# Expert stages that ask for their queries piecemeal, modulation kept as columns, decays by Relu on ScalarE

## The chip, the core and the metric

One core of one Trainium2 chip runs the whole program. The metric is device microseconds of one execution, from its first to its last instruction and what lies around them. TensorE is called PE, VectorE DVE, ScalarE ACT, GpSimd POOL; SP is the engine that issues most of the transfers. Everything is float32.

## What is computed

The reference chains two blocks over a sequence of 256 tokens of width 1024 (two tiles of 128 tokens, tt = 0 and 1 below). The first block has two layers of a hybrid mixer (four retention heads, and a state space part, SSD, with 32 heads in four groups) and a swiglu layer. The second block has two layers too; it has a second input, a context of 256 tokens:

```python
m_x = _modulation(c, w_mod[l], b_mod[l])                 # six rows of 1024: shift, scale, gate, twice
h = _modulate(x, norm1_g[l], m_x[0], m_x[1])             # rmsnorm(x) * g * (1 + scale) + shift
mix_x, _ = _token_mix(h, lp, ang, kv_c)                  # attention, Fourier and pooling branches
x = x + m_x[2] * mix_x
h2 = _modulate(x, norm2_g[l], m_x[3], m_x[4])
x = x + m_x[5] * _peer(h2, w_pq[l], peer_keys[l], peer_down[l], peer_up[l])
```

The context goes through the same in layer 0, and gives only keys and values in layer 1. `_peer` is the expert stage: eight query heads per token score 2 x 128 keys, the best 16 pairs of a head name 16 experts, and so a token has 128 experts; of each a row of `peer_down` (dotted with h2) and a row of `peer_up` (added up, weighted by gate times gelu of the dot product) are fetched. In the SSD part a head's decay matrix is exp(min(seg, 0)), seg being a difference of cumulative sums, times a masked product.

## The kernel before

`Plan.order` writes one list of items; each engine's program walks that list and emits its own part of every item, so an engine's instructions stand in the order of the list, and an engine that waits holds all that stands behind. Two streams are woven into the list. `x_stream` runs the first block, then for both layers of the second block `mix_phase` (modulation and token mix of x) and `peer_x` (expert stage of x). `context_stream` runs `modulation` (the product of c with `w_mod`, 48 MB), the context's `mix_phase` and its expert stage `peer_c`. Each generator yields an estimate of time, and `streams` takes the next item from the stream that is behind; at "alone" the context stream is emptied into the list. No instruction is moved at run time.

`modulation` (L635) adds up two rows per part in a PSUM bank, DVE adds the bias (L1813) and SP stores the rows to DRAM, in `mods` (L2356). `modulate` (L687) is called before each token mix and each expert stage: SP loads the norm gain, the scale and the shift as rows broadcast to 128 partitions (`mod_load`, L2366), DVE makes (1 + scale) * gain (L1819), and for either token tile multiplies by 1/rms and that gain (L1824) and adds the shift (L1826); PE turns the tile in blocks of 128 x 128 (L1214) and ACT copies four blocks at a time to `hT` (L2181). 1/rms comes by squares on ACT (L2081), a small step on DVE (L1615) and one on POOL (L2302). In the mixer, the rotation table is loaded behind `hT` (`load_cs`, L2370), and SP loads the first weights (wkv) behind that.

The first block's norms go by `stats`, `scaled`, `turn` (L313 to 326): squares, scaling on ACT (L2095), turning on PE (L1214) and a multiply on DVE into `hT` (L1623). PE fills the wait for them with products that nothing reads (`keep_busy`, L1224). `mix_out` adds the mixer's output to x on DVE (L1777), the second half of swiglu is added at L1790.

`heads` is the SSD part of one pair of heads: PE makes cumulative sums in a bank (L1300), DVE subtracts and takes the minimum with 0, three operations of 128 x 128 a head (L1706 to 1708), ACT takes the exponential (L2133), DVE multiplies by step and mask (L1713, L1714), PE multiplies by the inputs (L1290 to 1292). Each layer has 16 such pairs.

`peer_c` brings rows of one expert half at a time and uses DVE for both: dot products (`down`, L2013) and sums (`up`, L2024). `peer_x` first does all eight queries (`query`: 32 matmuls, L1179, then a copy by ACT, L2254) and scores (`score`, 8 matmuls, L1551; copies L2260 and L2261). Ranking (`rank`, L1909 to L1962, on DVE) makes one head's 16 indices. Then 256 steps follow, n = 128 tt + k: POOL fetches down and up row of expert k of each of the 128 tokens, 1 MB, into a ring place (L2315, q0 of the profile), DVE does the dot product (L2013); four steps make a batch, whose gelu is done at once (L1985 to L1992, L2269), ACT makes a diagonal matrix per expert (L2279) and PE adds the up rows by it in two banks (L1561, four matmul records per expert). A place comes free when its PE sums have ended. In layer 0 the ring has 11 places, of which the last three (wx[2], hT, keys) come free when all queries and scores have ended; in layer 1 it has 14. Beside the steps of layer 0, `context_keys` makes the context's keys and values for layer 1, in the steps from n = 60 on, one piece every ten.

```python
        for i in range(9):
            if i < 8:
                query(i, early[i] if i < 3 else None)
            if i:
                score(i - 1)
```

## Time and profile before

| what | value |
|---|---|
| time, median of 3 runs | 4311.15 us (4305.10 to 4315.73) |
| the profiled execution's time | 4306.61 us |
| its span | 4305.2 us |
| granted PE clock, mean | 0.938 |
| PE busy | 3722.5 us, 86% |
| DVE busy | 2369.1 us, 55% |
| POOL busy | 1300.6 us, 30% |
| ACT busy | 601.2 us, 14% |
| read from HBM | 1211.07 MB, 282 GB/s |
| first block | to about 2236 us |
| x, layer 0: token mix; expert stage | 2236 to 2548; 2548 to 3294 us |
| x, layer 1: token mix; expert stage | 3294 to 3577; 3577 to 4305 us |

Busy shares are over the whole span, and the stages differ: in the token mixes PE is nearly always busy, in the expert stages of x the transfers are. The time of a stage is read from the engine or queue that ends last in it. In rows of the timeline, what stands in brackets is how long the engine had been idle, and what released it.

### The profile page before, as it was taken

What the parts mean: (1) busy time and instruction counts of PE and PEld (TensorE: products, weight loads), DVE (VectorE), ACT (ScalarE), POOL (GpSimd) and SP (SyncE); (2) the same over time, 40 slices, a digit from 0 to 9 for tenths busy, and PEclk for the clock granted to TensorE, in tenths of its full rate; (3) what the DMA queues carried; (4) which work ended last, traced back from release to release, by engine and by line L of the source; (5) the groups of instructions that cost most, each with busy time, mean ns of one, the idle gap of its engine ahead of it and who ended that gap; (6) DMA issues with size and microseconds to landing.
All of it is one profiled execution on the core that took longest, in us unless ns stands there. A gap on an engine that the chain in (4) does not pass through costs nothing. (4 is left out here: it accounts for less than half of the span.)

```text
span 4305.2 us, 41073 instructions
## 1 busy us (share of the span) xinstructions
PE 3722.5 (86%) x14696; PEld 2637.1 (61%) x14696; DVE 2369.1 (55%) x5573; ACT 601.2 (14%) x1567; POOL 1300.6 (30%) x1125
## 2 busy tenths in 40 slices
PE   8978899997988679999988998877877999877777
PEld 6667788886847568887846775333334787333333
DVE  3542112367767876766762115777774122877875
ACT  1212100100001110000002101111111221111111
POOL 1100000001664445765640003444441001444442
PEclk9989999998998879999998999998998999899999
DMA  8652334333997769999962338999996235999997
GB/s 322 248 207 97 125 139 184 139 138 125 413 367 283 251 236 363 405 398 366 408 265 90 118 134 355 418 374 382 419 421 256 108 113 227 391 421 421 421 421 317
DMA packets 209546, 1214.93 MB, mean 282 GB/s; under 512 B 23889, under 2 KB 25041, under 8 KB 97729
## 3 DMA queue, kind: packets, MB, share of 16 engines
q0 software_dynamic: 154368, 855.71, 49.7%
q1 hardware_dynamic: 54976, 356.60, 21.9%
q8 instruction: 119, 1.95, 0.2%
q14 instruction: 83, 0.67, 0.0%
HBM read 1211.07 MB, written 1.15 MB: 282 GB/s over the span
## 5 line engine op out<-in xcount | busy, mean ns | idle before, releaser
L1179 PE MATMUL bank<-big 128*128 128x256 f32 (+3 forms) x9848 | 2144.1, 378 | 68.9 <-issue 14.8
L1179 PEld LDWEIGHTS bank<-big 128*128 128x128 f32 x9848 | 1836.8, 192 | 379.0 <-issue 91.8
L2315 POOL DMA_INDIRECT big<-in_pboth,big x1024 | 1230.1, 1201 | 1279.3 <-PE bank L1561 635.4
L1561 PE MATMUL bank<-big 128*128 128x512 f32 x2048 | 1007.6, 651 | 278.4 <-ACT big L2279 278.3
L2013 DVE CUSTOM_DVE_ANT_0 big<-big 128x1024 f32<-128x1024 f32 x768 | 926.9, 1224 | 334.7 <-DMA big<-in_pboth,big 331.0
L1561 PEld LDWEIGHTS bank<-big 128*128 128x128 f32 x2048 | 416.6, 208 | 866.5 <-issue 501.3
L2302 POOL TENSOR_TENSOR big<-big 128x1 f32<-128x1 f32 (+1 forms) x49 | 44.6, 912 | 1565.6 <-DVE big L1615 1565.5
L2024 DVE SCALAR_TENSOR_TENSOR big<-big 128x1024 f32<-128x1024 f32 x254 | 326.2, 1284 | 36.3 <-DMA big<-in_pboth,big 12.9
L2279 ACT ACTIVATE big<-big 128x128 f32<-128x128 f32 x512 | 164.8, 391 | 251.6 <-DVE big L1992 241.5
L1214 PE MATMUL bank<-big 128*128 128x128 f32 x572 | 97.9, 309 | 96.6 <-DVE big L1826 37.7
L1214 PEld LDWEIGHTS bank<-big 128*128 128x128 f32 x572 | 75.7, 161 | 117.2 <-issue 68.3
L2269 ACT ACTIVATE big<-big 128x4 f32<-128x4 f32 x128 | 26.4, 207 | 767.6 <-DVE big L1988 767.6
L1688 DVE SCALAR_TENSOR_TENSOR big<-big,bank 128x512 f32<-128x512 f32 x32 | 22.0, 687 | 188.3 <-ACT big L2121 188.3
L1891 DVE SCALAR_TENSOR_TENSOR big<-big,bank 128x512 f32<-128x512 f32 x36 | 24.8, 689 | 177.2 <-PE bank L1179 177.1
L1869 DVE TENSOR_REDUCE big<-bank 128x1 f32<-128x512 f32 (+1 forms) x48 | 28.9, 603 | 164.8 <-PE bank L1462 163.9
L1369 PE MATMUL bank<-big 128*128 128x512 f32 x256 | 112.5, 601 | 7.3 <-DVE big L1784 7.3
L1224 PE MATMUL bank<-big 128*128 128x256 f32 x296 | 73.9, 411 | 40.8 <-DVE big L1623 29.0
L1672 DVE SCALAR_TENSOR_TENSOR big<-bank,big 128x255 f32<-128x255 f32 (+1 forms) x144 | 62.8, 478 | 79.8 <-ACT big L2109 78.1
L1224 PEld LDWEIGHTS bank<-big 128*128 128x128 f32 x296 | 61.1, 209 | 52.2 <-DVE big L1623 29.7
L1369 PEld LDWEIGHTS bank<-big 128*128 128x128 f32 x256 | 49.1, 193 | 69.8 <-issue 61.8
L2081 ACT ACTIVATE big<-big 128x1024 f32<-128x1024 f32 x26 | 27.5, 1056 | 415.0 <-DVE big L1790 148.7
L1770 DVE SCALAR_TENSOR_TENSOR big<-big,bank 128x256 f32<-128x256 f32 x32 | 13.5, 421 | 125.0 <-PE bank L1179 125.0
(197 smaller groups left out, 2167.4 us busy)
## 6 DMA issues: line engine op xcount, KB each, us to landing
big<-in_w SPq DMA_DIRECT2D x104, 1024.0 KB, 7.3
big<-in_wmod POOLq DMA_DIRECT2D x48, 1024.0 KB, 9.1
big<-in_wgu SPq DMA_DIRECT2D x44, 1024.0 KB, 8.0
big<-in_wzg SPq DMA_DIRECT2D x36, 1024.0 KB, 4.8
big<-in_wro SPq DMA_DIRECT2D x32, 1024.0 KB, 6.8
big<-in_wpq SPq DMA_DIRECT2D x24, 1024.0 KB, 4.8
big<-in_wd SPq DMA_DIRECT2D x22, 1024.0 KB, 8.0
big<-in_pboth,big POOLq DMA_INDIRECT x1024, 12.4
```

What stands on the lines that cost most here:

```text
L1179: last = pe.matmul(o, a, b, start=(i == 0), stop=(i == n - 1))
L1214: last = pe.transpose(o[:, i, :], b, ident)
L1224: pe.matmul(u.ap[:, 0:256], ident, p.masks, start=True, stop=True)
L1369: last = pe.matmul(us[2 * tt + n].ap, act[:, 2 * i + k, tt * P:tt * P + P], wk[:, k, 512 * n:512 * n + 512], start=(i + k == 0), stop=False)
L1561: last = pe.matmul(u.ap, d.ap, row[:, 512 * i:512 * i + 512], start=(k == 0), stop=(k == 127))
L1672: i = v.scalar_tensor_tensor(c[:, m, s:256], o[:, m, 0:256 - s], conv["w"][m][:, 3 - s:4 - s], c[:, m, s:256], ALU.mult, ALU.add)
L1869: step(v.reduce_max(sm[:, c:c + 1], u.ap[:, 0:nk * P], AX.X))
L2013: v.tensor_tensor_reduce(row, row, h, 1.0, 0.0, ALU.mult, ALU.add, out).then_inc(done[0], 1)
L2024: v.scalar_tensor_tensor(at, s.ap, by, at, ALU.mult, ALU.add).then_inc(done[0], 1)
L2279: s.activation(d.ap, p.ident, ACT.Copy, scale=by).then_inc(diag[0], 1)
L2302: g.tensor_tensor(r.sm[:, 8 + r.at:8 + r.at + r.n], r.sm[:, 4 + r.at:4 + r.at + r.n], r.sm[:, 12:13].to_broadcast([P, r.n]), ALU.pow).then ...
L2315: g.indirect_dma_start(out=s.ap, out_offset=None, in_=table, in_offset=bass.IndirectOffsetOnAxis(ap=index, axis=0)).then_inc(s.full[0], 16)
```

## The change

1. **Expert stages of x.** Query 0, score 0 and query 1 are placed first, then the ranking of head 0 with its gates, then score 1, query 2, score 2. Queries 3 to 7 stand in front of the steps n = 8, 20, 32, 44 and 56, their scores in front of n = 10, 22, 34, 46 and 58. At n = 60, wx[2], hT and keys join the ring. In layer 0 four places are lent to the ring from the room of `context_keys`, and given back from n = 40 on; the pieces of `context_keys` come every twelve steps from n = 72. Two of the kernel's own places serve first as room for modulation rows. The ring has 11 places at the start of layer 0, 7 after n = 40 and 10 from n = 60 on, and 10, then 13, in layer 1.
2. **Last gates.** The last eight steps of a stage form batches of 2, 2, 2, 1 and 1 instead of two of 4.
3. **Modulation as columns.** `modulation` also turns each part by four blocks on PE (`mod_columns`) and keeps shift and gain as columns. `modulate` scales tile 0 by 1/rms on ACT and tile 1 on DVE, PE turns, and ACT and DVE each take four blocks of a tile with gain and shift as they copy to `hT`. The first norm needs no rows from DRAM. The expert stages still need rows of h2 for the dot products: they are loaded and made apart (`modulated_rows`), after the ranking of head 0 in x and after `hT` in the context. SP asks for keys ahead of them, and for the rotation table behind x instead of behind `hT`.
4. **Decays.** The three operations a head of DVE become ACT's Relu with scale -1, and the exponential has scale -1.
5. **Places in the list.** After `mix_out` and after the last add of swiglu, statistics, both turns and the scaling of tile 1 stand together, and the time that the stream yields comes behind them.

```diff
+    def modulate(self, banks, sm, X, l, vec, which, h, hT, room=None):
...
+        put("row_scale", src=X[:, 0, :], dst=h[:, 0, :], by=sm[:, 8:9], r=rs[0], done=done[0], ready=ready)
+        put("row_scale_v", src=X[:, 1, :], dst=h[:, 1, :], by=sm[:, 9:10], r=rs[1], done=done[1])
...
+        for tt in range(2):
+            us = [banks.take() for _ in range(2)]
+            put("col_turn", h=h[:, tt, :], us=us, dst=hT[:, :, tt * P:(tt + 1) * P], done=done[tt], gain=gain, shift=shift,
+                cols_ok=self.cols_ok, r=None if vec or tt else rs[0])
...
-            put("load_cs", cs=cs, done=tick("d_cs", 16), before=[hT_ok])
+            self.put("load_cs", cs=cs, done=cs_ok, before=[self.x_ok])
...
+        asking = ask()
+        route = ranks(asking)
+        for _ in range(3):
+            next(asking)
+        for _ in range(6):
+            next(route)
+        for _ in range(3):
+            next(asking)
+        rows_ok = yield from rows(hT_ok)
...
+        brief = [] if last else pairs[-len(spare):]
...
+                if slot in brief and n >= 40:
+                    brief.remove(slot)
+                    self.side_ok = done
...
+        ends = {(tt, k) for tt, k in steps if k % 4 == 3} | {(1, k) for k in (121, 125, 126)}
...
+            if n < 60 and n % 12 in (8, 10):
+                next(asking)
+            if n == 60:
+                for _ in asking:
+                    pass
+                asked_all()
...
-            if n >= 60 and n % 10 == 0:
+            if n >= 72 and n % 12 == 0:
...
-            v.tensor_scalar(d.ap[:, 0, :], pa.ap[:, o:o + 128], acs[:, 0, h:h + 1], 0.0, ALU.subtract, ALU.min)
+            s.activation(d.ap[:, 0, :], pa.ap[:, o:o + 128], ACT.Relu, bias=acs[:, 0, h:h + 1], scale=-1.0)
```

PE's order where the expert stage of layer 0 begins. wx0 to wx2 are the query weights' places, free4 and free5 the emptying of the banks, d_keys_x the keys' transfer. Before:

```order
L1179 MATMUL bank4<-big 128x256 [waits wx0,free4,free0]
L1179 MATMUL bank4<-big 128x256 x15
L1179 MATMUL bank5<-big 128x256 [waits wx1,free5]
L1179 MATMUL bank5<-big 128x256 x15
L1551 MATMUL bank4<-big 128x128 [waits free4,d_keys_x]
L1551 MATMUL bank4<-big 128x128 x3
L1179 MATMUL bank5<-big 128x256 [waits wx2,free5]
```

Now, in the change's own line numbers (L1257 is a query's product, L1634 a score's, L1644 the up sum):

```order
L1257 MATMUL bank4<-big 128x256 [waits free4,wx0,free0,free5]
L1257 MATMUL bank4<-big 128x256 x15
L1634 MATMUL bank5<-big 128x128 [waits free4,d_keys_x,free5]
L1634 MATMUL bank5<-big 128x128 x3
L1257 MATMUL bank4<-big 128x256 [waits wx1,free4]
L1257 MATMUL bank4<-big 128x256 x15
L1634 MATMUL bank5<-big 128x128 [waits free4,free5]
```

Score 0 stood behind query 1 and stands behind query 0. Before, five more queries and six more scores came ahead of the first up sum (L1561); now the fourth query comes behind four up sums, as the same engine's rows a little further on show:

```order
L1644 MATMUL bank0<-big 128x512 [waits pair2,diag_done]
L1644 MATMUL bank1<-big 128x512
L1644 MATMUL bank0<-big 128x512 [waits pair3,diag_done]
L1644 MATMUL bank1<-big 128x512
L1257 MATMUL bank4<-big 128x256 [waits wx0,free4]
L1257 MATMUL bank4<-big 128x256 x15
L1644 MATMUL bank0<-big 128x512 [waits pair4,diag_done]
```

DVE's order behind the last `mix_out` of the first block's second layer (L1777; full3 is its bank). L2024 are sums of the context's expert stage, L1623 the multiplies that empty the turned blocks. Before:

```order
L1777 SCALAR_TENSOR_TENSOR big<-bank,big 128x512 [waits full3]
L1615 TENSOR_SCALAR big<-big 128x1 [waits squares_done]
L2024 SCALAR_TENSOR_TENSOR big<-big 128x1024 [waits rows_read,row1,act_done_c]
L2024 SCALAR_TENSOR_TENSOR big<-big 128x1024 [waits rows_read,row2,act_done_c]
L2024 SCALAR_TENSOR_TENSOR big<-big 128x1024 [waits rows_read,row3,act_done_c]
L1623 TENSOR_TENSOR big<-bank,big 128x4x128 [waits full4]
L1623 TENSOR_TENSOR big<-bank,big 128x4x128 [waits full5]
```

Now (L1851 is `mix_out`, L1706 the multiply, L2133 the context's sum):

```order
L1851 SCALAR_TENSOR_TENSOR big<-bank,big 128x512 [waits full3]
L1698 TENSOR_SCALAR big<-big 128x1 [waits squares_done]
L1706 TENSOR_TENSOR big<-bank,big 128x4x128 [waits full4]
L1706 TENSOR_TENSOR big<-bank,big 128x4x128 [waits full5]
L1706 TENSOR_TENSOR big<-bank,big 128x4x128 [waits full4]
L1706 TENSOR_TENSOR big<-bank,big 128x4x128 [waits full5]
L2133 SCALAR_TENSOR_TENSOR big<-big 128x1024 [waits rows_read,row1,act_done_c]
```

The context's sums went from between the statistics and the two turns to behind both turns.

## Rows read from the trace of the kernel before

**Rows 1.** The page: rate of the transfers in 40 slices of 107.6 us.

```profile
GB/s 322 248 207 97 125 139 184 139 138 125 413 367 283 251 236 363 405 398 366 408 265 90 118 134 355 418 374 382 419 421 256 108 113 227 391 421 421 421 421 317
```

**Rows 2.** Windows of 10 us, expert stages: length, PE, PEld, DVE, ACT, POOL, clock, DMA share, GB/s.

```profile
2610.00:2620.00 10.00, 10.00 (x54) 8.90 (x54) 0.00 (x0) 1.70 (x4) 0.95 (x1) 1.00 1.02 422
2620.00:2630.00 10.00, 9.33 (x51) 8.14 (x50) 0.00 (x0) 2.64 (x9) 1.33 (x2) 1.00 0.21 72
...
2880.00:2890.00 10.00, 7.87 (x42) 5.27 (x41) 0.17 (x1) 1.06 (x6) 1.01 (x2) 1.00 0.52 216
...
2930.00:2940.00 10.00, 10.00 (x21) 4.38 (x20) 9.48 (x27) 1.59 (x6) 6.50 (x5) 0.84 0.61 213
...
3660.00:3670.00 10.00, 7.79 (x13) 3.46 (x14) 9.35 (x33) 1.28 (x4) 1.89 (x2) 0.66 0.76 277
```

**Rows 3.** Time to landing of the expert fetches: 2640 to 2860, 2585 to 2640, 3700 to 4250 us.

```profile
DMA to landing us min/median/max: 6.1/12.4/16.0
...
DMA to landing us min/median/max: 5.6/11.1/19.9
...
DMA to landing us min/median/max: 10.8/20.9/24.6
```

**Rows 4.** Timeline from the end of layer 0's token mix to the first fetch.

```profile
2548.31 1.06 ACT L2081 ACTIVATE big<-big 128x1024 f32<-128x1024 f32 x1 [37.16 <-DVE big L1905]
2560.83 1.97 PE L1214 MATMUL bank<-big 128*128 128x128 f32 x8 [5.88 <-DVE big L1826]
2565.69 14.14 PE L1179 MATMUL bank<-big 128*128 128x256 f32 x64 [0.68 <-ACT big L2181]
2581.51 0.29 DVE L1909 MAX8 big<-big 128x8 f32<-128x128 f32 x1 [18.28 <-ACT big L2261]
2591.81 1.00 POOL L2315 DMA_INDIRECT big<-in_pboth,big  x1 [40.03 <-DVE big L1962]
```

**Rows 5.** Timeline: layer 1's last two batches of up sums, and its last dot product.

```profile
4280.52 8.84 PE L1561 MATMUL bank<-big 128*128 128x512 f32 x16 [2.79 <-ACT big L2279]
4289.83 7.15 PE L1561 MATMUL bank<-big 128*128 128x512 f32 x16 [0.48 <-ACT big L2279]
...
4287.14 1.23 DVE L2013 CUSTOM_DVE_ANT_0 big<-big 128x1024 f32<-128x1024 f32 x1 [1.25 <-DMA big<-in_pboth,big]
```

**Rows 6.** Timeline: PE at the first weights of the token mixes of layers 0 and 1.

```profile
2264.28 5.40 PE L1179 MATMUL bank<-big 128*128 128x128 f32 x32 [5.48 <-DMA big<-in_wkv]
3305.15 1.90 PE L1214 MATMUL bank<-big 128*128 128x128 f32 x8 [4.56 <-DVE big L1826]
3314.59 5.88 PE L1179 MATMUL bank<-big 128*128 128x128 f32 x32 [4.95 <-DMA big<-in_wkv]
```

**Rows 7.** Timeline: PE's waits in the first block, behind the norms.

```profile
1032.23 6.14 PE L1224 MATMUL bank<-big 128*128 128x256 f32 x20 [15.43 <-DVE big L1623]
1285.06 6.01 PE L1224 MATMUL bank<-big 128*128 128x256 f32 x20 [7.61 <-DVE big L1623]
1992.19 7.42 PE L1224 MATMUL bank<-big 128*128 128x256 f32 x20 [5.96 <-DVE big L1623]
```

**Rows 8.** The SSD heads: lines of the page and of its groups by form, and PE's wait.

```profile
L1706 DVE TENSOR_SCALAR big<-bank,big 128x128 f32<-128x128 f32 x64 | 22.2, 346 | 38.4 <-PE bank L1300 33.2 <-DVE big L1696 3.8 <-issue 1.3
L2081 ACT ACTIVATE big<-bank 128x128 f32<-128x128 f32 x8 | 2.1, 273 | 34.6 <-PE bank L1179 34.6
L2279 ACT ACTIVATE big<-big 128x128 f32<-128x128 f32 x512 | 164.8, 391 | 251.6 <-DVE big L1992 241.5 <-PE bank L1561 10.0
1544.12 0.69 PE L1290 MATMUL bank<-big 128*128 128x64 f32 x2 [7.63 <-DVE big L1714]
1500.00:1600.00 100.00, 71.66 (x352) 63.03 (x352) 76.16 (x129) 17.11 (x35) 44.19 (x37) 0.80 0.70 238
```

**Rows 9.** Timeline: PE where the modulation has ended.

```profile
300.75 9.24 PE L1179 MATMUL bank<-big 128*128 128x256 f32 x32 [9.50 <-DMA big<-in_w]
314.08 1.07 PE L1214 MATMUL bank<-big 128*128 128x128 f32 x8 [4.09 <-DVE big L1826]
```

More of the change, by code:

```diff
@@ L503, in first_block @@
             yield from group_inputs(0, gots[0])
-            put("dt_sums", u=self.pa2.take(), dts=dts, ready=la_ok)
+            dts_ok = tick("dt_summed")
+            put("dt_sums", u=self.pa2.take(), dts=dts, ready=la_ok, done=dts_ok)
             for g in range(4):
@@ L647, in modulation, with part_end @@
         coming, late = [], []
+        def part_end():
+            l, part, args = late.pop()
+            put("mod_store", **args)
+            u = Use(banks.banks[(3 * l + part) % 2])
+            self.cols_ok = u.free
+            c4 = self.mcols[:, 2 * l:2 * l + 2, 16 * part:16 * part + 16].rearrange("p v (j b) -> p v j b", j=4)
+            gains = [(self.gcols[:, 4 * l + 2 * v + part // 2, :], self.mcols[:, 2 * l + v, 8 + 24 * (part // 2):16 + 24 * (part // 2)],
+                      self.col[l, "n2" if part else "n1"]) for v in range(2)] if part != 1 else []
+            put("mod_columns", src=args["rows"], u=u, ready=args["ready"], dst=c4, gains=gains)
         yield 30
@@ L650, in modulation @@
             for part in range(3):
-                s, b, u = st.take(), self.load(bm, t["bmod"][l, part], 512), banks.take(full=False)
+                s, b, u = st.take(), self.load(bm, t["bmod"][l, part], 512), Use(banks.banks[(3 * l + part) % 2], full=False)
                 put("mod_bias", ws=[b])
@@ L670, in modulation @@
                 rows = self.mods[l].rearrange("v a d -> v (a d)")
-                late.append(dict(dst=[rows[:, 2048 * part + 512 * j:2048 * part + 512 * j + 512] for j in range(4)],
-                    src=[s.ap[32 * j:32 * j + 2, :] for j in range(4)], ready=u.free, done=stored[turn]))
-        put("mod_store", **late.pop())
+                late.append((l, part, dict(rows=s.ap, dst=[rows[:, 2048 * part + 512 * j:2048 * part + 512 * j + 512] for j in range(4)],
+                    src=[s.ap[32 * j:32 * j + 2, :] for j in range(4)], ready=u.free, done=stored[turn])))
+        part_end()
         for w in few:
@@ L1086, in more, with lend, asked_all @@
             free.append(s)
-        while ar.size - ar.at >= 2048:
-            more(ar.get(2048))
+        for ap in places[:-2]:
+            more(ap)
         for ap in spare:
             more(ap)
+        brief = [] if last else pairs[-len(spare):]
         lent = []
-        for w in (self.wx[3], self.wx[4], self.wx[2]):
+        def lend(w):
             more(w.ap, w.freed)
             lent.append((w, pairs[-1]))
-        more(hT.rearrange("p a b -> p (a b)"), ended["hT"])
-        more(keys.rearrange("p a b -> p (a b)"), ended["keys"])
+        lend(self.wx[3])
+        lend(self.wx[4])
+        for ap in places[-2:]:
+            more(ap, rows_ok)
+        def asked_all():
+            put("load_row", dst=m5, src=self.mods[l, 0, 5:6, :].to_broadcast([P, 1024]), done=m5_ok, before=[ended["keys"]])
+            lend(self.wx[2])
+            more(hT.rearrange("p a b -> p (a b)"), ended["hT"])
+            more(keys.rearrange("p a b -> p (a b)"), ended["keys"])
         steps = [(tt, k) for tt in range(2) for k in range(128)]
@@ L1392, in mod, with mod_columns, col_turn @@
                              stop=(k == 7), tile_position=(0, 32 * j)).then_inc(done[0], 1)
-    def mod_turn(h, us, done, r=None, **_):
+    def mod_columns(src, u, ready, **_):
+        opened(u)
+        pe.wait_ge(*ready)
+        turn(u, [src[:, b * P:b * P + P] for b in range(4)]).then_inc(u.full[0], 1)
+    def col_turn(h, us, done, r=None, **_):
         for g, u in enumerate(us):
@@ L1406, in low_rank @@
         opened(u)
-        if ready:
-            pe.wait_ge(*ready)
+        for ok in ready or ():
+            pe.wait_ge(*ok)
         pe.wait_ge(*ws[0].full)
@@ L1538, in peer_q @@
     def peer_q(w, u, hT, ready, **_):
-        if ready:
-            pe.wait_ge(*ready)
+        for ok in ready or ():
+            pe.wait_ge(*ok)
         channel_chunk(u, w, hT)
@@ L2085, in halves, with row_stats, row_scale @@
         return [x[:, 0, :], x[:, 1, :]]
-    def row_stats(src, dump, r, ready):
+    def row_stats(src, dump, r, ready, room=None):
+        for ok in (ready, room):
+            if ok:
+                s.wait_ge(*ok)
+        squares(r, [src], [dump])
+    def row_scale(src, dst, by, r, done, ready=None):
         if ready:
             s.wait_ge(*ready)
-        squares(r, [src], [dump])
-    def row_scale(src, dst, by, r, done):
         s.wait_ge(*r.done)
@@ L2176, in mod_c, with col_turn @@
         s.activation(c3, c2, ACT.Tanh, scale=0.5).then_inc(tanh[0], 1)
-    def mod_turn(us, dst, **_):
-        for g, u in enumerate(us):
-            s.wait_ge(*u.full)
-            s.copy(dst[:, 4 * g:4 * g + 4, :], turned(u, 4)).then_inc(u.free[0], 1)
+    def col_turn(us, dst, gain, shift, cols_ok, **_):
+        u = us[0]
+        s.wait_ge(*cols_ok)
+        s.wait_ge(*u.full)
+        for k in range(4):
+            i = s.activation(dst[:, k, :], turned(u, 4)[:, k, :], ACT.Identity, bias=shift[:, k:k + 1], scale=gain[:, k:k + 1])
+        i.then_inc(u.free[0], 1)
     def low_rank(n, u, tmp, r, scaled, **_):
```

213 lines of the change are left out of this document (133 added, 80 removed).

## The prediction

> **What bounds the kernel now.** I read the page first. The transfers run at 421 GB/s in some slices of both expert stages of x and at 90 to 260 elsewhere [rows 1]: two of those slices are full, and nothing but fewer bytes or fewer gaps shortens them. So I cut these stages into windows of 10 us and looked for gaps [rows 2]. In layer 0 there is one at 2620 to 2630 us, where the rate falls to 72 GB/s, and the windows from 2880 to 2950 fall to between 213 and 398. Against 421 these cost about 9 us (with the window behind the first) and 21 us; small dips at 2790 and 2810 cost 3. In layer 1 the windows from 3650 to 3690 lose 8 us together, the worst stands in rows 2. Third, the landing times of the fetches [rows 3]: the shortest is 5.6 us with little queued, the median 12.4 us in layer 0 (11 places) and 20.9 in layer 1 (14). The three places more are 8.5 us, 2.8 a place, close to the 2.5 us that 1.05 MB take at 421 GB/s. What a landing takes above 5.6 us is the queue's reserve: 6.8 us in layer 0. Fourth, the way to the first fetch [rows 4]: 43.5 us from the end of the token mix (2548.3) to 2591.8, in which the transfers do little. Last, waits of PE outside these stages [rows 6 to 9], where PE is busy nine tenths of the time and a wait of PE is a loss unless the same place has another behind it.
>
> The sum is made against the profiled execution, 4306.6 us; the median of the runs is 4.5 us above it.
>
> **The way to the first fetch.** Before, squares end at 2549.5, the rows wait for their loads, hT is full at 2565.6, two queries of 7.1 us and a score pass before ranking starts at 2581.5, which takes 10.3 us [rows 4]. Now: squares and root of tile 0 to +2.1 us, ACT has the squares of tile 1 too (+2.7), scaling 1.1 (+3.8), eight turns 2.0, the same for tile 1, and four blocks copied at the end by ACT and DVE at 0.3 each: hT at +9.1 instead of +17.3, 8.2 us less. Score 0 stands behind one query: 7.2 less, 1.2 back for the copy between them that PE now waits for, 6.0 less. First fetch **14.2 us earlier** in each layer. DVE then makes the h2 rows in five operations of 1.25 us; the first row lands 5.6 us after its issue, so the first dot product is some 2 us late, and the ring covers that.
>
> **Behind the first fetch, layer 0.** The gap at 2620 was a full ring while PE worked off eight queries. It goes (9 us less), and ten route pieces in ten steps on DVE bring back some 2. Each query put between the steps takes PE 7.2 us and a score 1.1. A batch of four needs 7.15 us of PE at full clock [rows 5] per 10 us of transfers, so the batch behind a query starts 4.4 us late and the next but one is in time; the reserve of 6.8 us covers this. After n = 40 the ring has 7 places. Then one batch's places come free over 7 us, a fetch lands 5.6 us later, and the next batch closes only when the row behind it has been read: about 11.7 us a batch instead of 10. Five batches are 8.5 us, two of them with a query in front add 3.5: 12 more. From n = 60 there are 10 places against 11, so the two stalls by the context's keys (21 us) lose 2 more each: 4 more. Its three loads of 0.5 MB are gone: 3.7 less. Some weights now load behind the first fetch instead of before it, 1 MB: 2.5 more. Last gates: the last dot product ends at 4288.4 and PE at 4297.0 [rows 5]; with batches of 2, 2, 2, 1, 1 PE follows the rows at 1.8 us each and ends at about 4294, 3 less. Layer 0: 14.2 + 7 + 3.7 + 3 - 12 - 4 - 2.5 = **9.5 us less**.
>
> **Layer 1.** No places are given back; 10 places until n = 60 leave a landing of about 10.9 us, 5.3 above the shortest, still over 4.4. 14.2 + (8 - 2) + 3 - 2.5 = **21 us less**.
>
> **Start of the token mixes.** In layer 0 the order on DVE still has five of the context's sums and its last add in front, so only 3.3 us of the modulation go; the rotation table no longer holds wkv back, 5 of the 5.48 us wait: **8 us less**. In layer 1 [rows 6] x is ready at 3294.5 and PE starts at 3314.6; now hT is full at +9.1 and wkv, asked for at 3294.5, has landed: **11 us less**.
>
> **The first block's turns.** PE's bank is opened by L1623, which stood behind the context's work. Without that work DVE could have run it 6.5, 5.6 and 4.0 us earlier than it did in the three waits [rows 7]: **16 us less**. The context's work is only moved behind; DVE has room for it, at 60 to 70% busy there. If PE stands at the next bank instead, up to all of it comes back.
>
> **The decays.** 384 operations of 346 ns leave DVE [rows 8], 192 a layer. They overlap, and a pair of heads holds DVE for 1.9 us. In layer 0 DVE is half idle and I count nothing. In layer 1 PE waits four times for L1714, 2.4 to 7.6 us each; 2 of each and two waits of 1.5 us behind L1708 are 11 us. If DVE's own load set the pace, each of four groups would be shorter by what left it, 8 us, 33 in all. The windows there have DVE at 76 and PE at 72%: they wait for each other in turn. I take **20 us less**, between 11 and 33. What ACT takes on is hidden: it is 17% busy there. Its price for a Relu from a bank has no row; the nearest, a squares pass of the same shape from a bank, has 273 ns, and a scaled copy between SBUF places 391.
> The Trainium skill, ScalarE: Activation LUTs, section Rules for kernel authors, says of relu "Use VectorE, not ScalarE", since DVE is up to about three times as fast per element in bf16. The rows are of float32 from a bank, with 273 ns for ACT and 346 for DVE, so the trace does not agree for this shape. By the rule, a pair on ACT would take 5.7 us instead of 1.9, and 32 pairs 122 us more than now if nothing hid them.
>
> **The end of the modulation.** The weights for which PE waited 9.5 us [rows 9] stood behind three loads of 0.5 MB and are asked for 1.3 us earlier: 5 less. The context's rows, 4.1 and 1.4 us of waits: 5.5 less. 24 more turns on PE, at 1.1 to 2 us for eight: 4 more. **6.5 us less.**
>
> **Sum.** 9.5 + 21 + 8 + 11 + 16 + 20 + 6.5 = 92 us; 4306.6 - 92 = **4214 us**, own range 4190 to 4240.
>
> **Rivals.**
> *The ring is short.* For it: in layer 0 the reserve was once down to half a microsecond (shortest landing 6.1 against 5.6), and seven places are four fewer. Against: a median of 12.4. If each of ten insertions loses 3 us and the 20 steps with 7 places lose 30 instead of 12, the time is 4214 + 30 + 18 = **4262**.
> *The first block keeps its time.* The turns and decays only uncover the next wait (8.3 us for L1733 and 6 for the root stand beside them): 28 of the 36 us come back, **4242**.
> *Relu is the dearer.* At 391 ns a piece, unhidden, the pair loses 6 x 0.13 us against DVE's pace, 25 us over 32 pairs, and the 20 are lost: **4259**. The rule above points this way; the row of 273 ns speaks against it.
> *More than forecast.* Decays give 33, and the stalls by the context's keys lose nothing from the lost place and the 7 places nothing: **4185**.
> *Slower: PE becomes the bound of the first 60 steps.* Its place is the up sums with a query between them. At the lower level of the clock (1.2 GHz) a query takes 13.7 us, a score 2.2 and, at 8.84 us a batch [rows 5] (the batch that stands first there; part of it ran at that level, behind 2.8 us of idling), twelve steps 42 us against 30. It decides from the point where PE's twelve steps pass 30 us. Ten times 12.3 is 123 us more: 4214 + 123 = **4337**. Against it: the batch with little idling before it took 7.15 us, and PE with queries idles less, and in the window 2610 to 2620 with queries back to back the granted clock was 1.00.
> The Trainium skill, TensorE: Matmul & The Clock Gate, section What's actually happening, states that activity releases the throttle; the trace agrees, with a granted clock of 1.00 at 2610 and of 0.66 at 3660 [rows 2].
> That the change does not do what it says I leave out: the order on the engines shows it.
>
> **How the numbers follow.** Forecast 0.50, ring short 0.20, first block 0.12, Relu 0.03, more 0.11, slower 0.04. Of the time, 4175 to 4280 holds all but the slower case and the tails of the outer ones, about 0.85 by this count, a little under that for what I did not think of. A measurement of this kernel tells 0.3%, 13 us, from no change. All cases but the last are faster by more; a tail of the ring case, with twice its loss, comes to no change. Faster 0.92, same 0.04, slower 0.04.
>
> **What would show it.** First fetches some 14 us after the start of the stages less than before, 29 instead of 43.5 from the end of the token mix. No window under 300 GB/s between the first fetch and n = 40. Windows of 350 to 400 GB/s while there are 7 places. In layer 1, PE's product with wkv 9 us behind x. The waits for L1623 under 9, 3 and 3 us. PE at 80% instead of 72% in layer 1's heads. I am wrong if fetches land in 6 us over long stretches outside the seven-place steps, if PE's waits in the first block keep their sum under other names, or if the clock in the first 60 steps falls below 0.8.

## The result, and the profile after

The changed kernel takes **4274.4 us** (median; 4271.2 to 4276.1) where the kernel before takes 4312.2: ratio 0.9911, 95% interval 0.9895 to 0.9927, so 38 us faster, between 31 and 45. The forecast was 92 us, 4214 us in a range of 4190 to 4240. The profiled execution took 4274.6 us against 4306.6.

The page of the changed kernel, its busy times and its 40 slices of 106.8 us (transfers in GB/s):

```profile
PE 3683.7 (86%) x14648; PEld 2608.6 (61%) x14648; DVE 2322.7 (54%) x5464; ACT 658.6 (15%) x1800; POOL 1299.2 (30%) x1125
...
GB/s 325 236 198 106 120 148 169 146 117 144 413 370 312 265 254 386 405 402 386 411 231 62 137 206 383 308 384 311 403 416 300 108 114 262 380 402 420 420 420 336
```

Against [rows 1]: where slices 25 to 28 ran at 355, 418, 374 and 382, they run at 383, 308, 384 and 311. Layer 0's expert stage has holes that it did not have. Two marks of the timeline cut the program into stages: the squares passes that follow each sum into x, and the first expert fetch of each layer. Differences of these marks, in us (before and after are the profiled executions; the other rows are the experiments below):

| | mixer 0 | swiglu 0 | mixer 1 | swiglu 1 | token mix 0 | to first fetch | experts 0 | token mix 1 | to first fetch | experts 1 |
|---|---|---|---|---|---|---|---|---|---|---|
| before | 1003.9 | 263.2 | 705.2 | 264.0 | 312.0 | 43.5 | 702.7 | 281.2 | 43.5 | 679.9 |
| after | 1008.9 | 250.6 | 684.6 | 258.8 | 303.2 | 27.8 | 745.8 | 270.7 | 27.8 | 688.7 |
| forecast of the difference | -6.5 | -36 in these three | | | -8 | -14.2 | +4.7 | -11 | -14.2 | -6.5 |
| measured | +5.0 | -12.6 | -20.6 | -5.2 | -8.8 | -15.7 | **+43.1** | -10.5 | -15.7 | **+8.8** |
| e1, places back late | 1008.5 | 250.5 | 691.9 | 258.8 | 302.8 | 27.8 | 725.4 | 270.8 | 27.8 | 691.5 |
| e2, turns on ACT | 1006.9 | 250.6 | 689.1 | 260.5 | 303.4 | 27.8 | 728.1 | 270.9 | 28.1 | 689.1 |
| e3, score placed | 1010.0 | 250.6 | 688.4 | 258.8 | 302.8 | 27.8 | 734.5 | 270.8 | 27.9 | 683.5 |
| e4, Relu alone | 1006.3 | 264.5 | 696.9 | 263.5 | 314.6 | 43.7 | 703.6 | 282.7 | 45.4 | 680.7 |
| e5, decays on DVE | 1003.5 | 250.6 | 701.9 | 258.5 | 303.3 | 27.8 | 740.4 | 271.4 | 27.9 | 689.5 |
| e6, turns apart | 1009.0 | 263.0 | 698.9 | 266.5 | 309.6 | 27.8 | 741.2 | 271.0 | 27.9 | 689.7 |
| e7, three edits | 1006.8 | 250.6 | 687.7 | 258.8 | 303.2 | 27.9 | 699.6 | 271.8 | 28.1 | 682.2 |
| e9, Relu in layer 1 only | 1003.8 | 250.6 | 684.6 | 258.5 | 300.4 | 27.8 | 697.2 | 270.4 | 27.8 | 679.5 |
| e10, load ahead | 1006.0 | 258.7 | 695.3 | 258.7 | 307.6 | 27.8 | 698.1 | 272.7 | 27.9 | 682.4 |

(+4.7 is the forecast of -9.5 without the -14.2 that has its own column.) Outside the two columns of the expert stages the first mixer missed its forecast by 11.5 us, and the rest came near it; behind the first fetches 38 us were lost in layer 0 and 15 in layer 1 against it. Three views of the changed kernel show how.

**First**, windows of 10 us of layer 0 (columns as in [rows 2]), and the timeline around the hole:

```profile
2660.00:2670.00 10.00, 10.00 (x18) 4.27 (x19) 9.02 (x29) 0.94 (x4) 0.00 (x0) 0.71 0.44 184
2670.00:2680.00 10.00, 8.97 (x37) 6.62 (x36) 0.00 (x0) 1.76 (x5) 0.00 (x0) 1.00 0.00 0
...
2690.00:2700.00 10.00, 9.23 (x15) 4.04 (x16) 4.23 (x15) 1.28 (x4) 3.09 (x3) 0.68 0.55 205
...
2850.00:2860.00 10.00, 6.73 (x12) 2.98 (x13) 9.59 (x27) 2.85 (x10) 1.68 (x2) 0.66 0.31 107
...
2890.00:2900.00 10.00, 10.00 (x19) 4.16 (x18) 8.37 (x23) 1.64 (x7) 5.10 (x4) 0.78 0.42 136
```

```profile
2655.70 0.94 POOL L2442 DMA_INDIRECT big<-in_pboth,big  x1 [0.70 <-PE bank L1644]
2659.74 10.10 PE L1644 MATMUL bank<-big 128*128 128x512 f32 x16 [4.31 <-ACT big L2406]
2669.68 7.09 PE L1257 MATMUL bank<-big 128*128 128x256 f32 x32
2676.86 0.59 ACT L2381 COPY big<-bank 128x512 f32<-128x512 f32 x1 [13.31 <-PE bank L1257]
2677.35 1.27 ACT L2406 ACTIVATE big<-big 128x128 f32<-128x128 f32 x4
2677.80 7.15 PE L1644 MATMUL bank<-big 128*128 128x512 f32 x16 [1.03 <-ACT big L2406]
2680.06 0.94 POOL L2442 DMA_INDIRECT big<-in_pboth,big  x1 [23.42 <-PE bank L1644]
```

The sums that end at 2669.8 free four places, and all four are the lent ones, which go to nobody. The next batch waits behind a query on PE, and its diagonals (L2406) behind the query's copy (L2381) on ACT. POOL idles 23.4 us and the transfers stop. From there to n = 60 the first fetches of the batches stand at 2680.1, 2694.8, 2710.9, 2726.0 and 2741.3: 15 us a batch, where the forecast worked out 11.7.

**Second**, the gaps at 2850 and 2890, from the same timeline (this list ends at 2900.00, inside the sums that begin at 2889.22):

```profile
2842.83 1.37 DVE L1934 TENSOR_SCALAR big<-bank,big 128x128 f32<-128x128 f32 x4 [7.41 <-PE bank L1292]
2853.27 15.81 PE L1644 MATMUL bank<-big 128*128 128x512 f32 x32 [10.55 <-ACT big L2406]
2857.55 0.95 POOL L2442 DMA_INDIRECT big<-in_pboth,big  x1 [14.24 <-PE bank L1644]
...
2879.35 1.37 DVE L1934 TENSOR_SCALAR big<-bank,big 128x128 f32<-128x128 f32 x4 [6.91 <-PE bank L1292]
2889.22 11.01 PE L1644 MATMUL bank<-big 128*128 128x512 f32 x19 [9.99 <-ACT big L2406]
2893.28 1.95 POOL L2442 DMA_INDIRECT big<-in_pboth,big  x1 [13.70 <-PE bank L1644]
```

L1934 is DVE's half of the context's turned blocks. The turn (L1292) stands on PE behind a batch of sums, so DVE waits for PE with the next dot products queued behind; when they are done, PE has idled 10 us and POOL 14. Before, ACT alone emptied these banks.

**Third**, DVE's waits for ACT's tanh (L2396) in a batch's gelu, in layer 1:

```profile
3694.00 0.16 DVE L2101 SCALAR_TENSOR_TENSOR big<-big 128x4 f32<-128x4 f32 x1 [4.57 <-ACT big L2396]
3731.76 0.16 DVE L2101 SCALAR_TENSOR_TENSOR big<-big 128x4 f32<-128x4 f32 x1 [8.46 <-ACT big L2396]
```

The rows of ACT and PE just before the first of these two:

```profile
3692.12 1.05 PE L1634 MATMUL bank<-big 128*128 128x128 f32 x8
3693.21 0.37 ACT L2387 COPY big<-bank 128x256 f32<-128x256 f32 x1 [7.25 <-PE bank L1634]
3693.74 0.22 ACT L2396 ACTIVATE big<-big 128x4 f32<-128x4 f32 x1
```

ACT is not busy there: the copy of a score (L2387) stands ahead of the tanh and waits for PE, which has the query's delay and a batch of sums ahead of the score (L1634).

In the first block, the waits that answer to [rows 7], [rows 9] and [rows 8] (the list of rows ends at 300.00 for the row at 298.84, so its 1.62 us are part of the product):

```profile
1030.44 6.41 PE L1302 MATMUL bank<-big 128*128 128x256 f32 x20 [8.04 <-DVE big L1706]
1271.78 6.27 PE L1302 MATMUL bank<-big 128*128 128x256 f32 x20 [1.88 <-DVE big L1706]
1959.91 4.58 PE L1302 MATMUL bank<-big 128*128 128x256 f32 x20 [1.88 <-DVE big L1706]
...
298.84 1.62 PE L1257 MATMUL bank<-big 128*128 128x256 f32 x3 [3.92 <-DMA big<-in_w]
736.50 9.20 PE L1257 MATMUL bank<-big 128*128 128x256 f32 x32 [8.09 <-DMA big<-in_w]
...
1519.25 0.69 PE L1368 MATMUL bank<-big 128*128 128x64 f32 x2 [6.07 <-DVE big L1788]
```

The turns' waits fell by 17 us together, the weights' wait at the end of the modulation by 5.6, and a new one of 8.1 us stands at 736.5. The decays' wait fell from 7.63 to 6.07, and with the three others of its layer from 22.6 to 18.3 us together.

### The profile page after: what moved, and what is told of

It reads as the page before. It is cut to its first block and busy times, and to the rows that moved or that the text cites. A ratio compares the mean times of both kernels' runs of the same rounds, so it can differ in the third digit from the quotient of the medians.

```text
span 4273.1 us, 41154 instructions
## 1 busy us (share of the span) xinstructions
PE 3683.7 (86%) x14648; PEld 2608.6 (61%) x14648; DVE 2322.7 (54%) x5464; ACT 658.6 (15%) x1800; POOL 1299.2 (30%) x1125
## 5 line engine op out<-in xcount | busy, mean ns | idle before, releaser
L1257 PE MATMUL bank<-big 128*128 128x256 f32 (+3 forms) x9848 | 2143.7, 378 | 65.3 <-DMA big<-in_w 15.9
L1257 PEld LDWEIGHTS bank<-big 128*128 128x128 f32 x9848 | 1837.3, 192 | 379.1 <-issue 87.5
L1644 PE MATMUL bank<-big 128*128 128x512 f32 x2048 | 998.3, 645 | 323.2 <-ACT big L2406 322.0
L1644 PEld LDWEIGHTS bank<-big 128*128 128x128 f32 x2048 | 412.4, 206 | 895.6 <-issue 492.4
L2133 DVE SCALAR_TENSOR_TENSOR big<-big 128x1024 f32<-128x1024 f32 x254 | 326.1, 1284 | 36.9 <-DMA big<-in_pboth,big 14.1
L2406 ACT ACTIVATE big<-big 128x128 f32<-128x128 f32 x512 | 165.0, 391 | 239.8 <-DVE big L2101 234.7
L1292 PE MATMUL bank<-big 128*128 128x128 f32 x596 | 94.3, 294 | 75.3 <-ACT big L2208 24.9
L2396 ACT ACTIVATE big<-big 128x4 f32<-128x4 f32 (+2 forms) x134 | 27.7, 207 | 740.4 <-DVE big L2097 735.9
L1292 PEld LDWEIGHTS bank<-big 128*128 128x128 f32 x596 | 73.6, 152 | 96.6 <-issue 76.5
L1447 PE MATMUL bank<-big 128*128 128x512 f32 x256 | 110.6, 593 | 3.6 <-DVE big L1858 3.6
L1447 PEld LDWEIGHTS bank<-big 128*128 128x128 f32 x256 | 48.3, 189 | 65.0 <-issue 60.6
L1302 PE MATMUL bank<-big 128*128 128x256 f32 x224 | 58.3, 419 | 27.8 <-DVE big L1706 11.8
L2374 ACT ACTIVATE big<-bank,big 128x256 f32<-128x256 f32 x72 | 30.3, 472 | 287.4 <-PE bank L1257 287.4
```

The source lines that it names most:

```text
L1257: last = pe.matmul(o, a, b, start=(i == 0), stop=(i == n - 1))
L1292: last = pe.transpose(o[:, i, :], b, ident)
L1302: pe.matmul(u.ap[:, 0:256], ident, p.masks, start=True, stop=True)
L1447: last = pe.matmul(us[2 * tt + n].ap, act[:, 2 * i + k, tt * P:tt * P + P], wk[:, k, 512 * n:512 * n + 512], start=(i + k == 0), stop=False)
L1644: last = pe.matmul(u.ap, d.ap, row[:, 512 * i:512 * i + 512], start=(k == 0), stop=(k == 127))
L2133: v.scalar_tensor_tensor(at, s.ap, by, at, ALU.mult, ALU.add).then_inc(done[0], 1)
```

## Experiments

Ratios are to the kernel before on the same chip, with their 95% intervals; 0.001 is 4.3 us, and differences between kernels are taken from the ratios.

### e1: the lent places go back at n = 56

```diff
-                if slot in brief and n >= 40:
+                if slot in brief and n >= 56:
```

> The changed kernel, but the four lent places of layer 0 are given back at their first use from n = 56 on, not from n = 40 on, so the ring goes from 11 places to 10 and never has 7. Theory A (the ring of 7 is what costs): the changed kernel's windows from 2660 to 2740 us moved 1896 MB/s x 10 us where 421 x 80 would have moved 3368, so 35 us are lost there; of these about 5 stay for the two queries in between: 30 us less than the changed kernel, 4245. Theory B (PE with queries in between is the bound, the ring only shows it): less than 8 us, 4266 or more.

Measured: 4257.7 us, ratio 0.9869 (0.9854 to 0.9884), 18 us less than the changed kernel; experts 0 took 725.4 instead of 745.8. That lies between the theories, with their 30 us and under 8. The same stretch in both, 80 us long (first the changed kernel, then e1, which stands 6 us later):

```profile
2660.00:2740.00 80.00, 61.01 (x163) 32.66 (x164) 37.14 (x108) 10.52 (x35) 19.62 (x19) 0.84 0.62 237
```

```profile
2666.00:2746.00 80.00, 68.48 (x192) 35.95 (x192) 51.29 (x152) 12.64 (x43) 29.19 (x27) 0.96 0.89 348
```

At 421 GB/s the first loses 35 us (80 x (1 - 237/421)), the second 14. So giving four places back at n = 40 cost 21; the rest, which I had put at 5, remained with eleven places.

### e2: ACT empties the context's turned blocks

The first piece is DVE's, the second ACT's; `by_act` holds for the context's keys alone.

```diff
     def col_turn(us, dst, gain, shift, cols_ok, by_act, **_):
+        if by_act:
+            return
         u = us[1]
...
-        s.wait_ge(*u.full)
-        for k in range(4):
+        for g, u in enumerate(us if by_act else us[:1]):
+            s.wait_ge(*u.full)
+            for k in range(4 * g, 4 * g + 4):
```

> The changed kernel, but in the context's modulation beside layer 0's steps ACT copies all eight blocks of a tile, and DVE none. Theory A (DVE, which now waits for PE's turns with dot products queued behind it, is what stalls): the two waits of DVE for the turned bank, 7.4 and 6.9 us, go, and with them the two windows of 107 and 136 GB/s at 2850 and 2890: 12 to 15 us less than the changed kernel, about 4261. Theory B (ten places instead of eleven make these gaps): ACT then waits for the same turns with the tanh of a batch behind it, and nothing is won: 4270 to 4276.

Measured: 4260.6 us, 0.9884 (0.9867 to 0.9900), 12 us less; experts 0 took 728.1, 17.7 less. Theory A. The windows from 2850 on, 160 us long, in the changed kernel and then in e2:

```profile
2850.00:3010.00 160.00, 119.10 (x286) 53.07 (x286) 105.02 (x304) 27.38 (x85) 58.70 (x52) 0.86 0.80 317
```

```profile
2850.00:3010.00 160.00, 124.39 (x302) 54.81 (x301) 109.63 (x316) 29.07 (x91) 64.00 (x56) 0.90 0.89 360
```

That is 16 us of transfers, with the same ten places. The kernel before, with eleven, had 367 from 2840 to 3000, so the lost place is worth some 3 us at most (160 x 7/421); DVE's wait was the price.

### e3: the score in front of the next batch

```diff
-            if n < 60 and n % 12 in (8, 10):
+            if 0 < n < 60 and n % 12 in (8, 0):
```

> The changed kernel, but the score of a query stands in front of the next batch's up sums (n = 12, 24, 36, 48) instead of behind the sums of the batch that the query delays (n = 10, 22, 34, 46, 58); the last score comes at n = 60. Theory A (ACT's copy of the score holds the tanh of the batch behind it; DVE's waits for ACT of 5.8, 4.6 and 8.5 us in layer 1 are that): these waits fall under 3 us and 4 to 8 us are won in each layer, 4262. Theory B (it is PE's time for queries and sums that runs out): the waits turn into waits for PE, within 3 us of the changed kernel, 4271 to 4277.

Measured: 4257.7 us, 0.9869 (0.9854 to 0.9884), 18 us less; experts 0 by 11.3, experts 1 by 5.2. What ended DVE's idle time before L2101, over the whole program, in the changed kernel and in e3:

```profile
  ACT big L2396: 28.5, 8
```

```profile
  ACT big L2396: 0.5, 2
```

Theory A, with more in layer 0 than its 4 to 8 us. Five scores a layer, moved by two steps, are worth as much as the four places.

### e4: the Relu decays alone, in the kernel before

```diff
-            v.tensor_scalar(d.ap[:, 0, :], pa.ap[:, o:o + 128], acs[:, 0, h:h + 1], 0.0, ALU.subtract, ALU.min)
+            s.activation(d.ap[:, 0, :], pa.ap[:, o:o + 128], ACT.Relu, bias=acs[:, 0, h:h + 1], scale=-1.0)
```

> The kernel before with the fourth part of the change alone: the decays by Relu on ACT. My term for it was 20 us, 11 to 33 by its bounds. Theory A: 12 to 20 us less than before, all of it in layer 1's mixer, 4292 to 4300 (the changed kernel's first mixer of layer 1 is 20.6 us shorter, of which the row turns may be 5). Theory B (the layer's gain comes from the turns and from the order, the Relu gives little): less than 6 us, 4306 or more.

Measured: 4310.6 us, 0.9997 (0.9988 to 1.0006): no change. By the time this is theory B. In the profiled executions mixer 1 is 8.3 us shorter, mixer 0 2.4 longer, and the rest is lost by one to three microseconds a stage. The 8.3 us are two fifths of the forecast, and hardly more than that mixer differs from one execution to another of the same first block (684.6 to 691.9, see e5); whatever was won there does not reach the end.

### e5: the decays back on DVE, in the changed kernel

> The changed kernel with the fourth part taken back: DVE makes the three operations a head again. The Relu decays alone took nothing measurable from the kernel before (ratio 0.9997), though its layer 1 mixer was 8 us shorter. Theory A (the Relu is worth 8 us in that mixer and is paid back by what is woven beside it): 2 to 8 us more than the changed kernel, 4276 to 4282, with the waits for the decays in layer 1's heads at 7 to 7.6 us again instead of 6.1. Theory B (with the other parts in place the Relu is worth my 20 us): 4290 or more. Theory C (worth nothing at all): 4272 to 4276.

Measured: 4294.5 us, 0.9948 (0.9934 to 0.9962), 16 us more than the changed kernel, with an uncertainty of 9 from the two intervals. In its profiled execution mixer 0 is 5.4 shorter and mixer 1 701.9 us, against 684.6 to 691.9 in seven executions with the changed kernel's first block (its own, e1, e2, e3, e7, e8 and e11); the execution as a whole is 8 longer than the changed kernel's. So with the turns in their new place the Relu is worth more than alone, but the size stays loose, 8 us by the profiled execution and 16 by the timings: between A and B. PE's waits answer to A:

```profile
1456.18 0.69 PE L1368 MATMUL bank<-big 128*128 128x64 f32 x2 [7.63 <-DVE big L1797]
```

And the pieces themselves, in the changed kernel, by form (the first of the three Relu of a head, then the multiply on DVE of the same shape, which takes what the subtraction took):

```profile
L2251 ACT ACTIVATE big<-bank,big 128x128 f32<-128x128 f32 x64 | 23.8, 371 | 113.8 <-issue 73.6 <-PE bank L1378 40.2
...
L1788 DVE SCALAR_TENSOR_TENSOR big<-big 128x128 f32<-128x128 f32 x64 | 22.1, 346 | 0.0
```

A Relu from a bank takes 371 to 382 ns, not 273.

### e6: the turns apart again

The yields behind swiglu's last add are changed in the same way.

```diff
             r1 = stats(1, early)
+            yield 7
             turn(0, early, None, h0, self.col[l, "nffn"])
...
-            yield 9
+            yield 1.5
```

> The changed kernel with the fifth part taken back: the yields of the first block's norms stand between statistics and turns again. My term was 16 us in three waits. Theory A (worth what the waits show, 15.4, 7.6 and 6.0 before against 8.0, 1.9 and 1.9 in the changed kernel, 17 us): 4287 to 4293. Theory B (it only moves waits): 4272 to 4279.

Measured: 4312.0 us, 0.9993 (0.9983 to 1.0003), 35 us more than the changed kernel, with an uncertainty of 8. Theory A, and beyond it: the place is worth twice what the waits show. The three waits are back, 13.6, 7.6 and 7.4, and with them one that had stood in no list of mine, for swiglu's product on DVE:

```profile
1202.97 47.59 PE L1451 MATMUL bank<-big 128*128 128x512 f32 x104 [5.25 <-DVE big L1862]
```

(The list of rows ends at 1250.00, inside this product.) The wait was 5.65 before (L1784) and is 1.65 in the changed kernel (L1858). Swiglu 0 is 12.4 longer, mixer 1 some 10, swiglu 1 7.7, token mix 0 6.4. That the context's work of the whole stage then stands elsewhere in the list is my reading of the other waits; it was not tried apart.

### e7: e1, e2 and e3 together

> The changed kernel with three edits together: the lent places go back from n = 56 on, ACT alone copies the context's turned blocks, and the score stands in front of the next batch's sums. Alone they gave 17, 14 and 17 us. Theory A (three separate stalls): 40 to 48 us less than the changed kernel, 4226 to 4234. Theory B (all three feed the same short ring, and one of them mended leaves the others little): 4240 to 4255.

Measured: 4224.1 us, **0.9786** (0.9772 to 0.9799), 54 us less than the changed kernel by the ratios. Experts 0 took 699.6; the three gains there, 20.4, 17.7 and 11.3, add up to 49.4, of which 46.2 came. Theory A, and somewhat beyond its 40 to 48 us: three separate stalls. The stretch that had lost 35 us:

```profile
2660.00:2740.00 80.00, 70.48 (x200) 36.89 (x198) 57.80 (x170) 12.92 (x44) 33.77 (x29) 0.96 1.00 405
```

### e8: e7 with all queries first in layer 1

```diff
+        if last:
+            for _ in asking:
+                pass
+            asked_all()
...
-            if 0 < n < 60 and n % 12 in (8, 0):
+            if not last and 0 < n < 60 and n % 12 in (8, 0):
...
-            if n == 60:
+            if not last and n == 60:
```

> As the run with the three edits, but in layer 1 all eight queries stand behind the first ranking, ahead of the steps, so that the ring has 13 places at once. Theory A (ten places with queries between them suffice once the score is moved): layer 1 loses the time in which PE works off five queries and scores, about 45 us of PE against 13 places that hold 33 us of transfers, and saves under 5 us: 5 to 10 us more than the run with three edits. Theory B (ten places are too few in layer 1's first 60 steps, 19 us lost there in the changed kernel): 5 us or more less than it.

Measured: 4232.4 us, 0.9801 (0.9788 to 0.9815), 6 us more than e7; its experts 1 took 687.6 against 682.2. Theory A by the trace, though the intervals overlap. POOL waits for queries with a full ring:

```profile
3568.47 0.94 POOL L2449 DMA_INDIRECT big<-in_pboth,big  x1 [17.84 <-PE bank L1261]
3586.24 0.94 POOL L2449 DMA_INDIRECT big<-in_pboth,big  x1 [16.84 <-PE bank L1261]
```

So asking for all queries first is no better in layer 1 than asking piecemeal. Whether ten places are enough there it does not show, since its thirteen come with PE's delay.

### e9: e7 with the first layer's decays on DVE

`heads` takes a flag that holds in layer 1; without it DVE makes the three operations and the exponential has scale 1.

```diff
-                    put("heads", pa=pa, at=8 * g + j, dd=dd, dts_ok=dts_ok, seg=[tick("decay_log"), pa.free],
+                    put("heads", pa=pa, at=8 * g + j, dd=dd, dts_ok=dts_ok, by_act=l == 1, seg=[tick("decay_log"), pa.free],
```

> The run with the three edits (4224, ratio 0.9786), but in the first block's first layer DVE makes the decays again, and ACT only in the second. The first layer's mixer took 1003.5 us with all decays on DVE and 1006.8 to 1010 with them on ACT. Theory A (in the first layer, where DVE was half idle and the Exp of a pair already kept PE waiting, the Relu lengthens the chain by its pieces on ACT): 3 to 5 us less, ratio about 0.978, PE's waits for the decays at 187 and 253 us back to 2.4 from 3.0. Theory B (what that mixer lost is all in the weights' wait at 736 us): within 2 us.

Measured: 4215.1 us, **0.9765** (0.9746 to 0.9784). Mixer 0 took 1003.8, 3 less than e7 (and 1006.8 to 1011.8 in the seven executions with the Relu there), and its two waits are 2.45 and 2.39 as foretold; the wait at 732 stays 8.2. Theory A in the trace; the ratio is 9 us below e7's, but the two intervals overlap. It is the lowest ratio of all that ran.

### e10: e7 with one weights' load ahead

```diff
+        if vec:
+            yield 10
         put("load_iota", dst=iot, done=iot_ok, before=[ready])
```

> The run with the three edits, but one yield more in the context's stream ahead of its load of the index row, so that SP asks for one more of the first block's weights before it waits for the end of the context's token mix. Theory A (this queue order made PE's wait of 8.1 us at 736.5 us): the wait falls under 2 us and 6 to 8 us are won in the first layer's mixer, ratio about 0.977. Theory B (PE would wait for DVE or ACT at that place anyway, or the later context work costs as much): within 2 us of the run with the three edits.

Measured: 4239.0 us, 0.9806 (0.9788 to 0.9823), 9 us more than e7, with overlapping intervals, and not the 6 to 8 less of theory A. SP's order in the changed kernel: one weights' load stands behind the index row, which waits for the end of the context's token mix.

```profile
706.34 0.33 SPq L2460 DMA_DIRECT2D big<-in_wout  x1
728.59 0.33 SPq L2505 DMA_DIRECT2D big<-in_iota  x1
...
729.43 0.90 SPq L2460 DMA_DIRECT2D big<-in_w  x2
```

With the load in front the wait of 8.1 us is gone, so its cause is shown. But mixer 0 is 0.8 us shorter, not 7: PE waits 5.0 us for DVE later.

```profile
887.95 1.94 PE L1294 MATMUL bank<-big 128*128 128x128 f32 x8 [5.02 <-DVE big L1838]
```

The yield shifts all that is woven behind it too: swiglu 0 is 8 us longer, which among the runs with these turns only e12 shows too, with the same yield, and mixer 1 as much, of which 7 can be the difference between executions.

### e11: e7 with two last batches of four

```diff
-        ends = {(tt, k) for tt, k in steps if k % 4 == 3} | {(1, k) for k in (121, 125, 126)}
+        ends = {(tt, k) for tt, k in steps if k % 4 == 3}
```

> The run with the three edits, but the last eight steps of a stage form two batches of four again. My term was 3 us a stage, from the last dot product to PE's last sum. Theory A: 5 to 7 us more, half in each expert stage, ratio 0.980. Theory B (PE's cold clock on short batches takes the gain back): within 2 us.

Measured: 4228.7 us, 0.9784 (0.9767 to 0.9801): not told apart from e7. Its last sums, then those of e7 (the list of rows begins at 4199.64, inside its sums), each with the last dot product:

```profile
4209.99 7.15 PE L1644 MATMUL bank<-big 128*128 128x512 f32 x16 [1.22 <-ACT big L2409]
...
4207.29 1.23 DVE L2124 CUSTOM_DVE_ANT_0 big<-big 128x1024 f32<-128x1024 f32 x1 [1.26 <-DMA big<-in_pboth,big]
```

```profile
4199.64 14.78 PE L1644 MATMUL bank<-big 128*128 128x512 f32 x34
...
4207.75 1.23 DVE L2124 CUSTOM_DVE_ANT_0 big<-big 128x1024 f32<-128x1024 f32 x1 [0.97 <-DMA big<-in_pboth,big]
```

From the end of the last dot product to PE's last sum it is 8.6 us with batches of four and 5.4 with short ones: 3.2 us, where the forecast had 3, below what a timing can tell. Of the theories' sizes, 5 to 7 us or within 2, the ratio fits the second; the reason given there is not what the trace shows.

### e12: e9 and e10 together

> The three edits with both the decays of the first layer on DVE and the load ahead. Theory A (two separate losses of the first mixer, both real): 9 to 13 us less than the run with three edits, ratio about 0.976. Theory B (they stand one behind the other, only one is won): 3 to 8 us less, 0.977 to 0.978. Theory C: nothing, 0.9786.

Measured: 4234.8 us, 0.9801 (0.9784 to 0.9819), 6 us more than e7, with overlapping intervals. None of the three: mixer 0 took 1000.5, 6.3 less than e7, but swiglu 0 and mixer 1 took 256.5 and 695.8, 6 and 8 longer, much as in e10.

## Why the prediction was wrong

Right, each by its own column of the table: the way to the first fetch (14.2 forecast, 15.7 measured, twice), the starts of the token mixes (8 and 11; 8.8 and 10.5), and the last gates (3; 3.2 by e11). The first block gave 33 us in the profiled execution against 42.5, and 27 to 29 in e1 to e3, whose first block is the same: sizes were off both ways inside it, and that 33 or 28 is not farther from 42.5 is in part luck. The rival of PE as the bound did not come: the granted clock of the first 126 us behind the first fetch was 0.91, and the transfers ran at 402 GB/s. Of the signs named beforehand, windows of 350 to 400 GB/s with seven places did not come (184, 0 and 205 above), nor did 80% of PE in layer 1's heads: from 1475 to 1575 us it was busy 71%.

Wrong, the expert stages first:

1. **Seven places, "about 11.7 us a batch", 12 us.** Measured 15 us a batch and 21 us by e1. My count closed the next batch one landing after the first place was freed. It left out that 2.3 to 4.1 us pass from the start of a batch on PE to the first fetch into a place that it frees, that the fetch then takes 1 us to issue, and that the four places given back are one whole batch's, so that the first turn of the short ring has nothing in the queue: 23.4 us of POOL idle.
2. **The stalls by the context's keys, "4 more".** Not in the sum at all was DVE's wait for the turned bank, 7.4 and 6.9 us, 17.7 us by e2. The prediction prices such pieces only on the way to the first fetch, as work of 0.3 us each; the context's pieces beside the steps it does not price, neither as work nor as a wait with dot products queued behind it. This is the step that asks what stands behind a waiting instruction, left out for one part.
3. **"The reserve of 6.8 us covers this", for the queries.** PE's delay of 4.4 us was covered (402 GB/s in the stretch above). The score's copy on ACT, with the tanh behind it, was not looked at: 11.3 and 5.2 us by e3. In layer 0 the three terms make up what is missing: 9 (21 instead of 12), 17.7 and 11.3 are 38 us.
4. **The decays, 20 us.** Alone they are worth nothing measurable (e4), in the changed kernel 8 to 16 (e5), and in the first layer they cost 3 (e9). The term took 2 us off each of four waits of PE; together they fell by 4.3 us instead of 8, and PE's share in the heads did not rise. A piece takes 371 to 382 ns, not the 273 I took; the far end of the bound, 391, was nearer. The rival's 0.13 us a piece does not follow from the rows either: 391 less 346 is 0.045 us, 9 us over the 32 pairs and not 25. The count of 384 operations was wrong too: [rows 8] has 64 of one of three, 192 in both layers; the term did not use it. The rule that I weighed there, from the Trainium skill's page ScalarE: Activation LUTs, section Rules for kernel authors, to make relu on VectorE, points the right way for these pieces. In this trace the difference is 371 to 382 against 346 ns, in float32 from a bank, where the page has up to about three times in bf16. So what mixer 1 gains cannot come from a faster engine; that it comes from spreading the load is what is left, and was not tried apart.
5. **The turns, 16 us.** 35 by e6, of which 6.4 lie in token mix 0: this term was too small, and it hid some of the errors above. It is not to be added to e5's 8 to 16, for the two parts meet in mixer 1: that mixer took 705.2 us with neither, 701.9 with the turns alone (e5), 698.9 with the Relu alone (e6), and 684.6 to 691.9 with both. I had priced the three waits (17 us fewer, near the 16) and nothing else that moves when the context's work moves.
6. **The end of the modulation, 6.5 us.** The wait for the weights fell as forecast (9.5 to 3.9); the two of 4.1 and 1.4 us gave way to two of 1.3 and 1.7. But the Relu in mixer 0 cost 3 to 5, and another wait of 8.1 us came at 736.5. Removing this one made mixer 0 0.8 us shorter in e10 and 3.3 in e12 (against e9), so it cost little of its own.

So the expert stages' columns hold 54 us of the 60 that are missing, and e7 gives 46 and 6.5 of them back. With them layer 0 is 8 us better than forecast, but layer 1's column stays at 682.2 against 673.4: 8.8 us remain, and in e7 windows of 10 us between 3560 and 3720 still fall to between 320 and 384 GB/s. No run takes these apart, so whether ten places are too few there stays open. The rival "the ring is short" (4262) was the nearest in number and named one of the three stalls; it is not what happened in the other two. My first sign of being wrong, fetches landing in 6 us over long stretches, did not come (medians of 10.0 us from 2740 to 2850 and 15.5 from 3578 to 3800) and was the wrong place to look: the stop of 23 us shows in the idle time of POOL and in the windows.

## What to carry to other kernels

When work is cut in pieces and put between the steps of a stream, ask for every piece on every engine it touches what it waits for and what is queued behind it there. A copy or a multiply of a third of a microsecond held DVE for 5 to 8 us where it waited for a busy engine ahead of the stream's own work, and moving it, or giving it to another engine, cost nothing that the columns show. Places lent to a ring were better given back when others joined it than a whole batch at once in the middle. And where one list orders all engines by estimates, a yield is part of the price: the yields at two places moved 35 us here, and another removed the wait that it was meant for and won nothing.

## What was not expected of the hardware

A Relu of 128 x 128 from a bank with a bias by partition takes ACT 371 to 382 ns, against 273 for a square of the same shape from a bank in [rows 8]; DVE takes 346 for the same size. Whether the bias makes the difference to the square no run shows.

Also open are three small terms of layer 0, loads that went and came (3.7 and 2.5 us) and the ranking between the steps (2), which no run took apart; and what the timing of e5 holds beyond the 8 us of its profiled execution, and how much of e9's gain is more than its 3 us in mixer 0.
